# Feed-forward up projections: one 512-column matmul for high weight against high and low data, halves of the bank summed on VectorE

## What is computed

```python
def sqrelu_mlp(x, w_up, w_down):            # twice; x 256x2048, w_up 2048x8192
    h = jax.nn.relu(x @ w_up)
    return (h * h) @ w_down
...
def _conv_ffn(h, w_up, conv_w, conv_b, w_down):   # once; w_up 2048x(2*5632)
    a = h @ w_up
    a = lax.conv_general_dilated(a, ...) + conv_b   # 3 taps along the tokens, per feature
    gate, val = jnp.split(a, 2, axis=-1)
    return (jax.nn.silu(gate) * val) @ w_down
```

## Time and profile before

| | us |
|---|---|
| median of 3 runs | 3347.34 |
| lowest, highest | 3345.17, 3347.81 |
| the profiled execution's own time | 3348.26 |
| span of its instructions | 3346.5 |
| TensorE busy | 3271.2 (98%) |
| VectorE busy | 1957.5 (58%) |
| ScalarE busy | 1457.6 (44%) |
| mean granted TensorE clock | 0.991 |

### The profile page before, as it was taken

One profiled execution on the slowest core, in us unless ns is written; L12 is line 12 of the kernel. 1 busy time (PEld: TensorE's weight loads), 2 busy tenths in 40 slices (PEclk: granted clock), 3 DMA queues, 4 the chain that ended last, 5 costly groups with the idle time before them and its releaser, 6 DMA issues.

```text
span 3346.5 us, 54505 instructions
## 1 busy us (share of the span) xinstructions
PE 3271.2 (98%) x22384; PEld 3046.2 (91%) x22384; DVE 1957.5 (58%) x1662; ACT 1457.6 (44%) x1287; POOL 379.2 (11%) x543
## 2 busy tenths in 40 slices
PE   7999999999999999999999999989999999999998
PEld 7889999999989999989999999969887999999997
DVE  7756555555565444466555555577657666565656
ACT  4444444444444444444444444334654444444443
POOL 2201433233350000000000000005000000000000
PEclk9999999999999999999999999999899999999999
DMA  7555655655545544446555555544334555555553
GB/s 269 189 189 199 201 203 196 204 195 203 201 157 186 177 165 166 164 175 239 187 187 185 185 186 186 187 148 178 120 122 165 201 188 188 185 180 186 188 188 113
DMA packets 117687, 613.40 MB, mean 183 GB/s; under 512 B 14480, under 2 KB 45264, under 8 KB 47184
## 3 DMA queue, kind: packets, MB, share of 16 engines
q1 hardware_dynamic: 94640, 594.79, 49.6%
q10 hardware_dynamic: 22944, 17.10, 1.6%
HBM read 599.26 MB, written 12.58 MB: 183 GB/s over the span
## 4 chain that ended last, share of the span: by engine, by line
PE 94%; DVE 3%; ACT 2%; issue 1%; DMA 0%; SPq 0%; POOL 0%; DVEq 0%; ACTq 0%; POOLq 0%
PE ps L1915 19%; PE ps L1917 19%; PE ps L1916 19%; PE ps L1963 11%; PE ps L1964 11%; PE ps L1965 11%; DVE wlo L1088 1%; ACT whi L556 1%; PE ps L2042 0%; PE ps L2237 0%; DVE row_stats L1137 0%; PE ps L2153 0%; PE ps L2135 0%; ACT y_rms L609 0%; DMA raw<-weights 0%
## 5 line engine op out<-in xcount | busy, mean ns | idle before, releaser
L1088 DVE TENSOR_TENSOR wlo<-raw,whi 128x2048 fp32r<-128x2048 f32 (+2 forms) x572 | 1254.1, 2198 | 1091.4 <-ACT whi L556 1089.8
L556 ACT ACTIVATE whi<-raw 128x2048 fp32r<-128x2048 f32 (+2 forms) x572 | 1043.4, 1831 | 1543.4 <-PE ps L1917 993.2
L1915 PE MATMUL ps<-x_pair,whi 128*128 128x256 f32 x5104 | 1451.6, 284 | 32.8 <-DVE wlo L1088 19.0
L1916 PE MATMUL ps<-x_pair,whi 128*128 128x256 f32 x5104 | 1447.1, 284 | 0.0
L1917 PE MATMUL ps<-x_pair,wlo 128*128 128x256 f32 x5104 | 1447.0, 284 | 0.0
L1915 PEld LDWEIGHTS ps<-x_pair,whi 128*128 128x128 f32 x5104 | 982.3, 192 | 37.3 <-issue 28.6
L1916 PEld LDWEIGHTS ps<-x_pair,whi 128*128 128x128 f32 x5104 | 982.7, 193 | 1.6
L1917 PEld LDWEIGHTS ps<-x_pair,wlo 128*128 128x128 f32 x5104 | 982.4, 192 | 0.0
L1963 PE MATMUL ps<-whi,hid_hi 128*128 128x512 f32 x1280 | 499.7, 390 | 0.2 <-DVE resid L1126 0.2
L1964 PE MATMUL ps<-wlo,hid_hi 128*128 128x512 f32 x1280 | 498.4, 389 | 0.0
L1965 PE MATMUL ps<-whi,hid_lo 128*128 128x512 f32 x1280 | 498.1, 389 | 0.0
(11 more groups left out here) (354 smaller groups left out, 2547.5 us busy)
## 6 DMA issues: line engine op xcount, KB each, us to landing
raw<-weights SPq DMA_DIRECT2D x539, 1024.0 KB, 4.7
read_tab<-read_tables SPq DMA_DIRECT2D x2, 3072.0 KB, 10.3
raw<-weights SPq DMA_DIRECT2D x8, 640.0 KB, 9.5
drive_tables<-drive_out ACTq DMA_DIRECT2D x16, 256.0 KB, 6.0
read_tables<-c_wide ACTq DMA_DIRECT2D x32, 128.0 KB, 5.9
drive_tab<-drive_tables SPq DMA_DIRECT2D x4, 1024.0 KB, 7.5
x_in<-x_t SPq DMA_DIRECT2D x4, 512.0 KB, 6.6
resid<-x_rows ACTq DMA_DIRECT2D x1, 2048.0 KB, 14.4
```

The source lines that it names most:

```text
L556: act.activation(whi[:, s, 0:width], raw[:, s, 0:width], ACT.Copy).then_inc(hi_ready, 1)
L1088: dve.tensor_tensor(wlo[:, s, 0:width], raw[:, s, 0:width], whi[:, s, 0:width].bitcast(F32), ALU.subtract).then_inc(lo_ready, 1)
L1915: pe.matmul(o, w_hi, x_hi, start=first, stop=False)
L1916: pe.matmul(o, w_hi, x_lo, start=False, stop=False)
```

## The change

In the up projections of mlp0, mlp1 and ffn, and only there, the two products with `whi` become one matmul. `wide` streams `x_pair[:, :, k, :]` (256 columns of `xhi`, then 256 of `xlo`, which lie 16 KB further on) past `whi` into a whole bank of 512 columns, and `wlo` against `xhi` is added into the bank's first half. A step over k is now two matmuls, of 512 and of 256 columns, in place of three of 256. A tile thus fills a bank, whose two halves must be added: `sum_tile` on DVE, a `tensor_reduce` that reads the 512 columns and writes 256, into `hid` (mlp) or the new SBUF tile `up_sum` (ffn), and raises `tile_summed`.

A block's four tiles now lie in banks 0 to 3, so the next block reuses them tile by tile: `wide_block` waits before tile s for the sum of tile s of the block before. `wide_first` does what `block_first` did. ACT's `activate` takes ReLU from `hid` in place, once four tiles are summed; `conv_first` and `conv_rest` read `up_sum`. DVE makes each sum just ahead of the `lo1` of the same slot (`lo4_sum`, `lo4_first`, `group`). Since the up blocks now use banks 2 and 3 too, the small matmuls of a side job move from ahead of the down step into its middle, between its second and third chunk, and ACT's `table_out` moves behind the second of the four `hi1` of the following up block. In the last round ACT's `last_hi` now stands ahead of both.

```diff
             def mlp(name, tables=False):
...
                 def activate(g):
-                    wait_used(act, up_quad(q0, g, 2))
...
-                    act.activation(hid[:], block_ps(1 if first else 0), ACT.Relu).then_inc(block_free, 1)
+                    act.wait_ge(tile_summed, g * 4 + (WIDE[name] + 4))
+                    act.activation(hid[:], hid[:], ACT.Relu).then_inc(block_free, 1)
...
                 activate(n - 1)
-                if tables:
-                    table_out(n - 2)
                 split(n - 1, True)
+                for s in range(SLOTS):
+                    if tables and s == 2:
+                        table_out(n - 2)
+                    hi1(q0 + 2 * n - 1, s)
...
+            def sum_tile(out_, q, s, bank):
+
+                wait_used(dve, q, s)
+                dve.tensor_reduce(out_[:, s, :], ps[:, bank, :].rearrange("p (h t) -> p t h", h=2), axis=AX.X, op=ALU.add).then_inc(tile_summed, 1)
...
+            def lo4_sum(q, out_, q_up):
+
+                for s in range(SLOTS):
+                    sum_tile(out_, q_up, s, s)
+                    lo1(q, s)
...
+            def wide(o, w_hi, w_lo, k, first, last):
+
+                if first:
+                    pe.matmul(o, w_hi, x_pair[:, :, k, :], start=True, stop=False)
+                    pe.matmul(o[:, 0:T], w_lo, xhi[:, k, :], start=False, stop=False)
+                    return None
+                pe.matmul(o[:, 0:T], w_lo, xhi[:, k, :], start=False, stop=False)
+                return pe.matmul(o, w_hi, x_pair[:, :, k, :], start=False, stop=last)
...
+            def wide_block(q, summed_, tables=None):
+
+
+                for s in range(4):
+                    pe.wait_ge(tile_summed, summed_ + s)
+                    if tables is not None and s == 2:
+                        pe.wait_ge(job_copied, tables)
+                        pe.wait_ge(lags_copied, tables)
+                    wide_tile(q, s, s, 1)
...
-            def down(q, u, hidden):
+            def down(q, u, hidden, between=None):
 
                 pe.wait_ge(hidden_lo, hidden)
                 for s in range(SLOTS):
+                    if s == 2 and between is not None:
+                        between()
                     chunk(q, s)
...
                 def rest(g):
-                    if tables:
-                        pe.wait_ge(block_free, g + (b0 + 3))
+                    def job():
+                        pe.wait_ge(tile_summed, g * 4 + (w0 + 8))
                         ssm_tables(g)
-                    down(g * 2 + (q0 + 2), g * 8 + UNITS[name], g + (h0 + 1))
+                    down(g * 2 + (q0 + 2), g * 8 + UNITS[name], g + (h0 + 1), job if tables else None)
```

More of the change, by code:

```diff
@@ L72 @@
 HIDDEN = {"mlp0": 0, "mlp1": FF // HID, "ffn": 2 * FF // HID}
+WIDE = {"mlp0": 0, "mlp1": FF // P, "ffn": 2 * FF // P}
+FIRST_BANKS = {"mix0": (2, 0, 3, 1), "mix1": (2, 0, 3, 1), "ffn2": (0, 2, 1, 3)}
+FIRST_ORDER = (0, 2, 1, 3)
 FEATURES = (("pool_scale", DT), ("ln_mix_g", 2 * DT), ("ln_mix_b", 2 * DT), ("ln_mlp_g", 2 * DT), ("ln_mlp_b", 2 * DT),
@@ L233, in build @@
         gate_sig = at("gate_sig", 68, [P, 4, T])
+        up_sum = at("up_sum", 32, [P, 2, 4, T])
         qkv_t = at("qkv_t", 48, [P, N_GROUPS, 3, T])
@@ L699, in mlp @@
                 activate(n - 1)
-                if tables:
-                    table_out(n - 2)
                 split(n - 1, True)
+                for s in range(SLOTS):
+                    if tables and s == 2:
+                        table_out(n - 2)
+                    hi1(q0 + 2 * n - 1, s)
                 if tables:
                     inner_store(n - 2)
-                hi4(q0 + 2 * n - 1)
-                if tables:
                     row_sqrt(name, 0, "ln_eps")
@@ L1235, in rescale, with lo4_first @@
                 rescale_bias(name + "_b")
+            def sum_tile(out_, q, s, bank):
+                wait_used(dve, q, s)
+                dve.tensor_reduce(out_[:, s, :], ps[:, bank, :].rearrange("p (h t) -> p t h", h=2), axis=AX.X, op=ALU.add).then_inc(tile_summed, 1)
+            def lo4_first(name, out_, q):
+                banks = FIRST_BANKS[name]
+                sum_tile(out_, q, 0, banks[0])
+                lo1(q + 1, 0)
+                sum_tile(out_, q, 2, banks[2])
+                sum_tile(out_, q, 1, banks[1])
+                lo1(q + 1, 1)
+                lo1(q + 1, 2)
+                sum_tile(out_, q, 3, banks[3])
+                lo1(q + 1, 3)
+            def lo4_sum(q, out_, q_up):
+                for s in range(SLOTS):
+                    sum_tile(out_, q_up, s, s)
+                    lo1(q, s)
             def add_down(q, nb):
@@ L1724, in conv_rest @@
                         o = conv[:, 4 * half_ + nt, lag:T]
-                        ins = dve.scalar_tensor_tensor(out=o, in0=block_ps(half_)[:, nt, 0:T - lag],
+                        ins = dve.scalar_tensor_tensor(out=o, in0=up_sum[:, half_, nt, 0:T - lag],
                                                        scalar=fcol("ffn_conv_w_2", i + tap * (2 * FF2 // P)), in1=o,
@@ L1733, in conv_rest, with group @@
                 dve.wait_ge(conv_done, g * 2 + (half_ + 1))
-                dve.sem_inc(block_free, 1)
-            def group(g, q, adds, last=False):
+            def group(g, q, q_up, adds, last=False):
+                gate_sum, value_sum = up_sum[:, 0], up_sum[:, 1]
                 conv_rest(g, 0)
+                sum_tile(value_sum, q_up, 0, 0)
                 lo1(q, 0)
@@ L1764, in group @@
                     split(hid_hi, hid_lo)
-            lo4(q0 + 1)
-            group(0, q0 + 2, False)
+            lo4_first("ffn2", up_sum[:, 0], q0)
+            group(0, q0 + 2, q0 + 1, False)
             with dve.Fori(0, n - 2) as g:
                 step.enter(g, 9)
-                group(g + 1, g * 3 + (q0 + 4), True)
-                lo4(g * 3 + (q0 + 6))
+                group(g + 1, g * 3 + (q0 + 4), g * 3 + (q0 + 3), True)
+                lo4_sum(g * 3 + (q0 + 6), up_sum[:, 0], g * 3 + (q0 + 5))
                 step.leave(n - 2)
-            group(n - 1, q0 + 3 * n - 2, True, True)
+            group(n - 1, q0 + 3 * n - 2, q0 + 3 * n - 3, True, True)
             def finish_rows(tt):
@@ L1926, in tile, with wide_tile, wide_first @@
                 return ins
+            def wide(o, w_hi, w_lo, k, first, last):
[5 more added lines that the diff above has]
+                return pe.matmul(o, w_hi, x_pair[:, :, k, :], start=False, stop=last)
+            def wide_tile(q, s, bank, n_used):
+                chunk(q, s)
+                for k in range(DT):
+                    c = slice(k * P, k * P + P)
+                    ins = wide(ps[:, bank, :], whi[:, s, c], wlo[:, s, c], k, k == 0, k == DT - 1)
+                ins.then_inc(chunk_used, n_used)
+            def wide_block(q, summed_, tables=None):
[5 more added lines that the diff above has]
+                    wide_tile(q, s, s, 1)
+            def wide_first(name, q, free):
+                pe.wait_ge(block_free, free)
+                banks = FIRST_BANKS[name]
+                for p in range(4):
+                    pe.wait_ge(norm_lo, LO0[name] + p + 1)
+                    for s in (0, 2):
+                        if p == 0:
+                            chunk(q, s)
+                        for k in range(4 * p, 4 * p + 4):
+                            c = slice(k * P, k * P + P)
+                            ins = wide(ps[:, banks[s], :], whi[:, s, c], wlo[:, s, c], k, k == 0, k == DT - 1)
+                        if p == 3 and s == 0:
+                            ins.then_inc(chunk_used, 1)
+                wide_tile(q, 1, banks[1], 2)
+                wide_tile(q, 3, banks[3], 1)
             def quad_tile(q, set_, s, slot, n_used, x_ready=None, order=range(DT)):
@@ L2059, in mlp @@
                     rest(g)
-                    quad_block(g * 2 + (q0 + 3), 0, g + (b0 + 4))
+                    wide_block(g * 2 + (q0 + 3), g * 4 + (w0 + 5), g + 2 if tables else None)
                 rest(n - 2)
```

41 lines of the change are left out of this document (24 added, 17 removed).

## The result

The changed kernel takes 3319.7 us (median of 4 runs, 3316.1 to 3325.0), the kernel before 3347.6 (4 runs, 3345.2 to 3350.0): a ratio of 0.9918, 95% interval 0.9901 to 0.9935. So it is 0.8% faster, where 1.2% had been forecast, and 3319.7 lies above the range (3299.0 to 3317.5). The profiled execution took 3324.99 us with a span of 3323.2; it is the longest of the four.

A forecast was written before the change was run, and what follows sets the result against it. TensorE's own matmul stream was taken as the bound. From the profiled 3348.26 us, 46.1 saved on matmuls, plus 0.1 low clock, 4.1 stall and 0.9 clock loss, gave 3307.3, median 3306.4; range 3299.0 to 3317.5.

The forecast's parts named there:

- What bounds the kernel: Whole kernel: TensorE's own stream, busy 98% of the span and 94% of the chain; nobody holds it up inside feed-forwards.
- The matmuls: Up blocks: 3456 steps each lose one fixed part of 13.33 ns, 46.1 us less; a step becomes 346.67 ns.
- Rival 2: Up blocks: the two-run operand costs half of what is saved, 6.7 ns a step; 3329.4 us, chance 0.05.
- The two-run operand at nothing: 512-column matmuls of the up blocks: streaming two runs 16 KB apart was taken to cost nothing.
- The clock in the denser stream: Up blocks: the denser matmul stream needn't slow the clock; granted 1.00, apart from 0.1 us at low-clock block starts.
- The formula of the Trainium skill: N/2.4 + 2.5 ns per warm matmul, a saving of only 8.6 us; set aside in favour of the trace's distances.
- The sums on VectorE: Up blocks: 216 sums of 0.68 us, 147 us more on VectorE, 58% to 63%, costing TensorE nothing.
- the bound of 3.0 us: ffn loop: VectorE would become the bound only from 3.0 us a sum.
- The side job: mlp0's last job: copies at 12.8 us, GpSimd's end 25.1 later; TensorE waits 4.1 us, plus 0.9 for lowered clock.
- rival 1: mlp0's last side job doesn't stall because GpSimd's chain is shorter; without 4.1 and 0.9, 3301.4 us, chance 0.12.
- The sum: Whole kernel: all terms together give 3307.3 us for the profiled execution, 3306.4 as median, 1.2% faster.
- the first item: Sign in the profile after: starts in an up block alternate by 120 and 227 ns; otherwise the prediction is wrong.

The follow-up runs named there:

- e2_all512: Changed kernel with the low weight also meeting all 512 columns, so every matmul of a tile has one width: 3666.5 us, one execution.
- e1_adjacent: Changed kernel with high and low data of each k side by side, so a 512-column matmul streams one run: 3319.6 us.
- e2_long_sum: Changed kernel with each of the 216 VectorE sums reading its bank four times over: 3339.1 us, one run.
- e4_job_late: Changed kernel with ScalarE's copies for mlp0's last side job moved behind the split of chunk 2: 3328.8 us, one execution.

## Why the prediction was wrong, point by point

**What bounds the kernel**: right. TensorE's own stream, 94% of the chain, and no waits.

**The matmuls**: this is the step that failed, by a size. The term was 3456 x 13.33 ns = 46.1 us. It rested on "a step becomes 120.0 + 226.67 = 346.67 ns", two distances that were each read from a stream of one width and added for a stream that mixes them. Each is right by itself: `e2_all512` has 226.6 ns in the up block. Mixed, the step is 353.3 ns and the tile 5.647, so 216 tiles x (5.760 - 5.647) = 24.4 us came back. 21.7 us of the forecast are missing here, 4 us more than the whole miss in the profiled execution (3325.0 against 3307.3); the stall that didn't come goes the other way. Rival 2, with half of the saving lost, had this size (6.7 ns a step; it was 6.7 in the alternation and 6.2 over the tile) and the wrong mechanism: `e1_adjacent` takes the two runs away and changes nothing. Nor was "within a run and across instructions the columns come at the clock rate" true across instructions of two widths. The rows that would have shown it were in the trace of before, at the head of each down step; and the check by the loop's period took "1.36 us for the side job" as what was left over, so it could not catch 0.02 us.

**The two-run operand at nothing**: right (`e1_adjacent`, `e2_all512`). **The clock in the denser stream**: right, tiles are alike through all three stages.

**The formula of the Trainium skill** ("TensorE: Matmul & The Clock Gate", Back-to-back issue gap), 109.2 and 215.8 ns, would have saved 8.6 us; 24.4 were saved. The Trainium skill gives that formula, in that section, for the isolated gap of a single matmul; the figure it has there for a sustained stream at 512 columns, about 131 ns, is not what the rows show either (226.67). It was right to go by the row, and wrong to think that the row covered the mix.

**The sums on VectorE**: right in duration (0.68 forecast, 0.69 measured), in share (63%) and in cost (no wait names them), and the bound of 3.0 us was not tested: at 2.29 us (`e2_long_sum`) no loop is longer, but the starts of the stages are.

**The side job**: half right. The copies came at the forecast 12.8 us; the chain behind them was taken over as a constant, 25.1 us, from one row of before. It was 19.4 and 21.2 in two profiles of the changed kernel, since it starts when its DMAs have landed (5.1 and 8.3 us behind the copies, 8.6 before) and is 2.1 us longer for each split of VectorE that it meets whole. In one execution 1.6 us were left, in the other TensorE waited 0.24 us; in all twelve traces that have the copies at this place the chain ended 19.4 to 21.3 us behind them, and TensorE waited 0.3 us at most. So rival 1 held: the forecast 4.1 + 0.9 us were about nothing. Where a stall did come (`e4_job_late`), the clock fell behind it to 0.50 and cost some 2 us, more than the 0.9 and the 1.7 of the prediction.

**The sum**: in the profiled executions 46.1 - 24.4 = 21.7 too little saved, 5.0 us of stall and clock that did not come, leaves 16.7 of the 17.7; the last 1.0 is not accounted for, and is less than what executions differ by. The prediction took "the first item" as what would prove it wrong, starts that alternate by 120 and 227 ns; that is what did.

## What to carry to other kernels

A distance between matmuls read from a stream of one shape holds in a stream of that shape. Where an edit mixes two, bound the mix apart, or order the matmuls so that equal widths stand in pairs or in one long row (not in fours, which gave back only a third of the loss); here that took the saving in matmul time from 24 us to 40 (216 x (5.760 - 5.573)) with the same instructions. If the trace at hand has a place where one stream follows the other, read the distances just behind it, not only in the middle. A chain of another engine that a stall is computed from is not a constant either: take it apart into what it waits for and what it runs beside, and compare its rows in several rounds before carrying its length over.

## What the runs showed of the hardware that was not expected

- Alternating 512- and 256-column fp32r matmuls: 353.3 ns a step, where uniform streams give 226.67 and 120.0. A change from 256 to 512 is paid with 28 ns over five matmuls (233, 236, 228, 233, 231 ns), a change back returns 8 ns. Groups of four lose more per tile (66 ns) than pairs (26) or one group of sixteen (20).
- A moving operand in two runs 16 KB apart, and where in the bank the narrow product lands: no difference.
- A reduction of 128x512 from PSUM into 128x256 takes 0.69 us, one that reads four times as much 2.29.
- GpSimd's tensor operations of 0.45 us take 2.5 when they begin just behind a 128x2048 subtraction of two SBUF operands on VectorE (2.29 us).
- One and the same program had granted clock 0.50 in one execution and 1.00 in another for 13 us at the head of the attention stage, worth 7 us. The whole spread of its first four times is 9 us; what the unprofiled ones owe to the clock is not shown beyond their mean granted clock, which goes from 0.990 in the longest to 0.993 in the shortest.
